# A decoder layer's expert product: output turned, 32 tokens taken by gathers, other packets for gates and activations

## The reference, cut to what matters

```python
idx = take(i1, ci // K) * 128 + take(i2, ci % K)         # (token, head, 16)
gate = softmax(sc)
act = gelu(einsum('thed,td->the', u_table[idx], xb))
y = einsum('the,thed->td', gate * act, v_table[idx])
x = x + y
```

## Time and profile before

| | us |
|---|---|
| median of 3 runs | 1489.33 (1485.82 to 1491.83) |
| the profiled execution | 1488.56 |
| its span | 1486.4 |
| TensorE busy | 1458.1 |
| VectorE busy | 1165.9 |
| ScalarE busy | 640.8 |
| GpSimd busy | 681.1 |

### The profile page before, as it was taken

One profiled execution on the slowest core, in us unless ns is written; L12 is line 12 of the kernel. 1 busy time (PEld: TensorE's weight loads), 2 busy tenths in 40 slices (PEclk: granted clock), 3 DMA queues, 4 the chain that ended last, 5 costly groups with the idle time before them and its releaser, 6 DMA issues.

```text
span 1486.4 us, 23381 instructions
## 1 busy us (share of the span) xinstructions
PE 1458.1 (98%) x8069; PEld 1301.4 (88%) x8069; DVE 1165.9 (78%) x2372; ACT 640.8 (43%) x1055; POOL 681.1 (46%) x394
## 2 busy tenths in 40 slices
PE   7999899999999999999999999999999999999998
PEld 6879668888999999999999999888888888888887
DVE  4747563388989999988998888578788778878876
ACT  4463472321433333467777666433332243233221
POOL 2423171233777768865545453134334434433341
PEclk9999999999999999999999999999999999999999
DMA  7400211312689999999999999699999999999993
GB/s 265 149 29 1 113 45 32 114 58 71 192 296 330 317 332 354 417 356 363 371 376 362 356 368 389 218 392 383 379 355 343 354 348 352 346 348 349 354 344 121
DMA packets 183962, 410.29 MB, mean 276 GB/s; under 512 B 12852, under 2 KB 108852, under 8 KB 182360
## 3 DMA queue, kind: packets, MB, share of 16 engines
q1 hardware_dynamic: 142296, 258.46, 49.3%
q0 software_dynamic: 41600, 151.03, 26.9%
HBM read 361.12 MB, written 48.30 MB: 275 GB/s over the span
## 4 chain that ended last, share of the span: by engine, by line
PE 75%; DVE 9%; DMA 9%; POOL 4%; issue 2%; ACT 1%; SPq 0%; DVEq 0%; ACTq 0%; POOLq 0%
PE banks L1996 17%; PE banks L1764 16%; PE banks L2065 12%; PE banks L2064 12%; PE banks L2066 12%; DMA u_rows<-in_u,idx 8%; DVE gate_rows L1623 3%; POOL u_lo L746 3%; DVE u_rows L1568 2%; POOL u_rows L762 2%; DVE u_lo L1551 1%; PE banks L1976 1%; DVE oh L1619 1%; PE banks L1791 1%; PE banks L1836 1%
## 5 line engine op out<-in xcount | busy, mean ns | idle before, releaser
L794 POOL DMA_INDIRECT v_rows<-in_v,idx x128 | 204.2, 1595 | 325.2 <-DVE x_res L1707 273.6
L2064 PE MATMUL banks<-v_hi,w_hi 128*128 128x512 f32 x768 | 298.8, 389 | 0.0
L2066 PE MATMUL banks<-v_hi,w_lo 128*128 128x512 f32 x768 | 298.8, 389 | 0.0
L2065 PE MATMUL banks<-v_lo,w_hi 128*128 128x512 f32 x768 | 298.8, 389 | 0.0
L1125 ACT ACTIVATE v_hi<-v_raw 128x1024 fp32r<-128x1024 f32 x128 | 126.3, 1050 | 326.1 <-PE banks L2066 298.5
L762 POOL DMA_INDIRECT u_rows<-in_u,idx x160 | 189.8, 1186 | 138.7 <-DVE z L1568 107.4
L1645 DVE TENSOR_TENSOR v_lo<-v_raw,v_hi 128x1024 fp32r<-128x1024 f32 x128 | 153.5, 1221 | 96.5 <-ACT v_hi L1125 96.3
L746 POOL TENSOR_TENSOR u_lo<-u_raw,u_hi 128x1024 fp32r<-128x1024 f32 x66 | 163.8, 2485 | 87.6 <-ACT u_hi L1011 53.7
L1996 PE MATMUL banks<-h_lo,u_hi 128*128 128x352 f32 x1024 | 196.1, 326 | 0.0
L1996 PE MATMUL banks<-h_hi,u_hi 128*128 128x352 f32 x1024 | 188.3, 326 | 0.0
L1996 PE MATMUL banks<-h_hi,u_lo 128*128 128x352 f32 x1024 | 184.7, 323 | 3.3 <-DVE u_lo L1551 3.3
(11 more groups left out here) (276 smaller groups left out, 2078.1 us busy)
## 6 DMA issues: line engine op xcount, KB each, us to landing
u_raw<-in_uT SPq DMA_DIRECT2D x128, 512.0 KB
v_raw<-in_v SPq DMA_DIRECT2D x128, 512.0 KB
gate_scratch<-stage SPq DMA_DIRECT2D x12, 2048.0 KB
gates<-gate_scratch SPq DMA_DIRECT2D x29, 768.0 KB
act_scratch<-act_out SPq DMA_DIRECT2D x116, 176.0 KB
act_in<-act_scratch SPq DMA_DIRECT2D x29, 704.0 KB, 7.4
wi_raw<-in_w_in SPq DMA_DIRECT2D x8, 1024.0 KB, 6.7
wq_raw<-in_w_q SPq DMA_DIRECT2D x8, 1024.0 KB, 6.0
```

The lines of the kernel that those rows point to most:

```text
L794: nc.gpsimd.indirect_dma_start(v_rows[s % V_ROWS][:], None, v_flat, bass.IndirectOffsetOnAxis(ap=idx0[:, s:s + 1], axis=0)).then_inc(vg_in ...
L2064: mm(y, w, v_hi[q][:, j, ds], start=first and j == 0, stop=False)
L2065: mm(y, w, v_lo[q][j][:, ds], start=False, stop=False)
L2066: end = mm(y, w_lo[q][:, j, t * P:(t + 1) * P], v_hi[q][:, j, ds], start=False, stop=last and j == GROUP - 1)
```

## The change

The second product is turned. Before, a matmul had 128 tokens of `w` as the stationary operand and 512 columns of v as the moving one, and gave tokens by width. Now 128 columns of v are stationary and 352 tokens of `w` move, and each of 8 banks holds one eighth of the width by tokens. At the end ScalarE copies the banks to `yT`, TensorE transposes them, and VectorE adds them to the residual.

The 32 tokens leave the dense part: 32 more tiles of v rows are gathered (kind "w"), scaled and accumulated in `acc_b`, four slots of a token in four partition groups, and `fold` sums these groups in eight matmuls into the first 32 columns of the banks. Gates are made for 352 tokens in 88 batches and 11 chunks, and the scaling of the gate table is gone, as is the save of the 32 tokens' chunk in the second product.

All gathers form one order (`ORDER`: dots a and b, then w, then v), with row tiles by address: 3 in turn for the first 12 tiles of v rows, then 6. The first four w tiles are added between the last blocks' splits, the other 156 tiles over groups 1 to 30, five or six a group.

Gates come in pairs of groups (1,024 bytes a piece), into `gate_pairs`, from the group `KEPT` on. Activations are saved by two blocks and loaded as pieces of 2,816 bytes. In the main stage VectorE makes the one-hot rows of all batches and five of the eight gate rows of two batches; ScalarE makes the other three, as a Square and a Relu each, with the gate as bias and the negated gate (`neg_g`) as scale. The output of the three token tiles leaves in six half tiles instead of three whole ones.

```diff
-BATCHES = ND // BATCH
+BATCHES = NA // BATCH
...
+for _n in range(POST + 4, E_BLOCKS):
+    DOTS[_n] = "w" * POST_ADDS
...
+ALL_DOTS += "w" * (NE - ALL_DOTS.count("w")) + "v" * SLOTS
...
+def adds_of(g):
+    return g * ADDS_LEFT // ADD_GROUPS - (g - 1) * ADDS_LEFT // ADD_GROUPS if g <= ADD_GROUPS else 0
...
+        WIDE, MAIN, POST_KB, LATE = (110, 114, 195, 199, 38, 42, 46, 50), (110, 114, 195, 199), (150, 110, 114), (134, 138, 177)
...
+            def save_acts(i, body, pair):
+
+                half = pair % 2
+                sp.wait_ge(act_ready, i * body + (2 * pair + 2))
+                sp.dma_start(act_d[bass.ds(i * (body // 2) + pair, 1)].rearrange("o p n t -> (o p) (n t)"),
+                             act_out[:, 2 * half:2 * half + 2, :].rearrange("p n t -> p (n t)")
+                             ).then_inc(act_saved[half], 16)
...
+            sp.wait_ge(tri_ready, 2 * (TB - 1) + 1)
+            for y in range(P // NE):
+                sp.dma_start(g1[y * NE:(y + 1) * NE, :], tri[0:NE, 0, 0, y * NE:(y + 1) * NE]).then_inc(g1_in, 16)
...
+            def load_pair(block, m, count=2 * GROUP):
+                sp.dma_start(gate_pairs[m][:, :, 0:count, :].rearrange("p c n t -> p c (n t)"),
+                             gate_d[:, :, bass.ds(block, count), :].rearrange("c p n t -> p c (n t)")
+                             ).then_inc(pairs_in[m], 16)
...
+                if s == U_DOTS:
+
+                    pool.wait_ge(gate_saved[1], 16 * (CHUNKS // 2))
+                if s == U_LATE:
+
+                    pool.wait_ge(z_done, E_BLOCKS)
...
-                for w in range(BATCH):
-                    at_t = tab[:, 2, bass.ds(token(i, b, w), 1)]
-                    nc.scalar.activation(oh2[:, slot, w, :], iota, ACT.Square, bias=at_t, scale=-1.0
+                for w in range(ROWS_DVE, BATCH):
+                    at_t = tab[:, 1, bass.ds(token(i, b, w), 1)]
+                    nc.scalar.activation(gate_rows[:, slot, w, :], iota, ACT.Square, bias=at_t, scale=-1.0
...
-                nc.scalar.activation(oh2[:, slot, :, :], oh2[:, slot, :, :], ACT.Relu, bias=1.0, scale=-1.0
-                                     ).then_inc(oh_scalar, 1)
+                for w in range(ROWS_DVE, BATCH):
+                    t = bass.ds(token(i, b, w), 1)
+                    last = nc.scalar.activation(gate_rows[:, slot, w, :], gate_rows[:, slot, w, :], ACT.Relu,
+                                                bias=tab[:, 0, t], scale=neg_g[:, t])
+                last.then_inc(oh_scalar, 1)
...
+            for c in range(KD):
+                act.wait_ge(y_done, c + 1)
+                copy(yT[:, c, :], ps[:, Y_BANKS[c], 0:ND]).then_inc(yT_ready, 1)
...
+                if kind == "w" and x == 0:
+                    nc.vector.tensor_scalar(acc_b[:], rows[:], z1[:, 0:1], None, ALU.mult).then_inc(dot_done, 1)
+                    return
+                w, into = (z1, acc_b[:]) if kind == "w" else (z0, x_res[:, 0, :])
+                nc.vector.scalar_tensor_tensor(out=into, in0=rows[:], scalar=w[:, x:x + 1], in1=into,
+                                               op0=ALU.mult, op1=ALU.add).then_inc(dot_done, 1)
...
-                if n % 2 == 0:
-                    nc.vector.tensor_tensor(oh2[:, slot, :, :], bc(iota, 1, BATCH),
-                                            bc(tab[:, 2, t0:t0 + BATCH], 2, NK), ALU.is_equal).then_inc(oh_ready, 1)
-                for t in range(t0, t0 + BATCH):
+                t0 = n * BATCH + NE
+                nc.vector.tensor_tensor(oh2[:, slot, :, :], bc(iota, 1, BATCH),
+                                        bc(tab[:, 2, t0:t0 + BATCH], 2, NK), ALU.is_equal).then_inc(oh_ready, 1)
+                for t in range(t0, t0 + (ROWS_DVE if n % 2 else BATCH)):
...
-                        step(nc.vector.transpose(z1t[:], z1[:]))
-                        settle()
-                        step(nc.vector.tensor_tensor(tab[:, 0, 0:NE], tab[:, 0, 0:NE], z1t[:], ALU.mult))
...
-            dve.wait_ge(dot_done, len(ORDER))
+            dve.wait_ge(dot_done, U_DOTS)
             weights(0, 0)
+            post_dots(POST + 4)
             split_u(POST + 5)
             split_w(0, 0)
+            post_dots(POST + 5)
             split_u(POST + 6)
+            post_dots(POST + 6)
             split_u(POST + 7)
...
-                for o in range(6):
-                    t, half = divmod(o, 2)
...
+                for c in range(KD):
...
+                    if last and c == 6:
+                        turn(0, range(4))
+                    if last and c == 7:
+                        turn(1, (4, 5))
+                    ds = slice(c * P, (c + 1) * P)
+                    y = ps[:, Y_BANKS[c], NE:ND]
                     for j in range(GROUP):
...
+                        mm(y, v_hi[q][:, j, ds], w_hi[q][:, j, :], start=first and j == 0, stop=False)
+                        mm(y, v_hi[q][:, j, ds], w_lo[q][:, j, :], start=False, stop=False)
+                        end = mm(y, v_lo[q][j][:, ds], w_hi[q][:, j, :], start=False, stop=last and j == GROUP - 1)
...
+            pe.wait_ge(dot_done, U_DOTS + NE)
+            for c in range(KD):
+                mm(ps[:, Y_BANKS[c], 0:NE], acc_b[:, c * P:(c + 1) * P], fold[:], start=False, stop=False)
             second(GROUPS - 1, 1, last=True)
```

More of the change, by code:

```diff
@@ new lines, in second @@
+                if not isinstance(p, int) or KEPT <= p + 2 < GROUPS:
+                    load_act(p + (2 - KEPT), q)
+            for p in range(4):
+                second(p, p % 2, p)
+            with sp.Fori(1, GROUPS // 4 - 1) as i:
+                for r in range(4):
+                    second(i * 4 + r, r % 2, r)
+            for p in range(GROUPS - 4, GROUPS):
+                second(p, p % 2, p % 4)
+            sp.wait_ge(dot_done, GATHERS)
+            sp.dma_start(a["out"][0:P, :], x_res[:, 0, :]).then_inc(out_saved, 16)
@@ L679, in _ @@
+            for o in range(6):
+                half, t = o // 3, 1 + o % 3
+                ds = slice(half * 512, (half + 1) * 512)
+                sp.wait_ge(y_added, o + 1)
+                sp.dma_start(a["out"][t * P:(t + 1) * P, ds], x_res[:, t, ds]).then_inc(out_saved, 16)
+            sp.wait_ge(out_saved, 16 * 7)
         @block.gpsimd
@@ L1099, in main @@
                     n = i * MAIN_BODY + (PRE + j)
-                    take_gates(i, 2 * j, first)
-                    if not (last and j == MAIN_BODY - 1):
+                    if not last or i * MAIN_BATCHES + 2 * j < BATCHES:
+                        take_gates(i, 2 * j, first)
+                    if not last or i * MAIN_BATCHES + 2 * j + 3 < BATCHES:
                         one_hot(i, 2 * j + 3)
@@ L1648, in weights @@
             def weights(g, q):
[L1649 removed]
+                if g < KEPT:
+                    dve.wait_ge(gates_in[q], (g - q) * 8 + 16)
+                    gate = gates[q][:]
+                else:
+                    m, half = divmod(g - KEPT, 2)
+                    dve.wait_ge(pairs_in[m % 2], m // 2 * 16 + 16)
+                    gate = gate_pairs[m % 2][:, :, half * GROUP:(half + 1) * GROUP, :]
                 if g:
@@ L2041, in main, with turn @@
                                 lambda b=b: gate_matrices(i, b, first and b < 4))
-                               for b in BATCHES_IN[j]]
+                               for b in BATCHES_IN[j] if not last or i * MAIN_BATCHES + b < BATCHES]
                     first_product(i * MAIN_BODY + (PRE + j), j, i, PRE + j, MAIN_BODY, between=between)
             main(0, True)
-            with pe.Fori(1, MAIN_TRIPS) as i:
+            with pe.Fori(1, MAIN_TRIPS - 1) as i:
                 main(i)
+            main(MAIN_TRIPS - 1, last=True)
             for n in range(POST, E_BLOCKS):
                 first_product(n, n, 0, n, 1, ring=2)
+            def turn(half, chunks):
+                for c in chunks:
+                    pe.wait_ge(yT_ready, max(c + 1, 3 * half + 3))
+                    for t in range(3):
+                        o = ps[:, Y_BANKS[3 * half + t], c % 4 * P:(c % 4 + 1) * P]
+                        end = nc.tensor.transpose(o, yT[:, c, t * P:(t + 1) * P], ident)
+                        if c % 4 == 3:
+                            end.then_inc(yT_turned, 1)
             def second(g, q, first=False, last=False):
```

248 lines of the change are left out of this document (115 added, 133 removed).

## The result

The kernel became slower by about half a per cent: 1499.59 us, median of 16 runs (1491.73 to 1503.77), against 1490.36 for the kernel before (16 runs, 1485.82 to 1497.13) on the same chip. The ratio is 1.0058, 95% interval 1.0044 to 1.0073. I had forecast 1462 with a range of 1448 to 1482: wrong in sign, and outside the range. The median lies 4.8 us above the profiled execution, where the forecast allowed 0.8; the profiles don't show what the slower executions add.

A forecast was written before the change was run, and what follows sets the result against it. TensorE and DMA were both near full in the second product, with DMA taking over as limit after the change; 1486.4 - 7.1 + 2 - 35.9 + 8 + 5.4 = 1458.8 us of span, forecast 1462, range 1448 to 1482.

The forecast's parts named there:

- the DMA limit of the second product: Second product: DMA queues at 395 GB/s, 15.9 us a group, start group 31 8 us later than TensorE's pace; bounds 0, 24.
- Case 2: Second product: DMA, VectorE and row buffers hold each other up; 1477 at 16.0 us a group, 1486 at 16.3; chance 0.2.
- Case 1: Second product: TensorE sets the pace throughout, larger packets lift the DMA ceiling to 412 GB/s; 1454 to 1446; chance 0.2.
- Case 3: Second product: slower through row-tile turnaround from 19.5 us on, 1503, or a 358 GB/s ceiling, 1521; chance 0.1.
- Second product turned: Second product: 96 matmuls at 158.3 ns, 15.20 us a group, 35.9 us less if TensorE sets the pace.
- Stage with gates, -7.1: First product with gate matrices: 88 batches instead of 96 at 0.89 us, 7.1 us less; bounds nothing and 14.6.
- Last eight blocks, +2: First product's last eight blocks: extra VectorE work ahead of u_lo, +1.4 and +0.6 us; bounds 0 and 6.
- End, +5.4: Kernel's end: fold 0.8 us, transposes inside the last group 2.3, longer tail after the last matmul 2.3; bounds 4 and 8.
- Conditions named for failure: Second product: below 382 GB/s means a mis-sized ceiling; forecast fails if first groups stand long or gaps reach 2.6 us.

The follow-up runs named there:

- Experiment 4: Changed kernel with 20 of the 160 row tiles added behind the last group: 1478.66 us, ratio 0.9917 to the kernel before.
- Experiment 5: Changed kernel without the product of v_hi with w_lo, 64 matmuls a group instead of 96, all bytes kept: 1486.97 us, ratio 0.9983 to the kernel before.
- experiment 3: Changed kernel with five row buffers instead of six in the second product: 1495.94 us, ratio 1.0048 to the kernel before.
- Experiment 6: Changed kernel with each two-group gate load made as two transfers, packets of 512 bytes instead of 1 KB: 1528.62 us, ratio 1.0269 to the kernel before.
- experiment 1: Changed kernel loading v blocks of the second product in half their width from the second group on: 1469.76 us, ratio 0.9863 to the kernel before.
- experiment 2: Changed kernel with 28 row tiles of v, every fifth, replaced by tiny transfers, all adds kept: 1472.57 us, ratio 0.9882 to the kernel before.
- experiment 11: Changed kernel with all gathered u row tiles from the fifth block with gates on replaced by 32-byte-a-partition transfers: 1481.97 us, a single execution.
- experiment 7: Changed kernel with 16 of the 160 row tiles added behind the last group: 1481.60 us, ratio 0.9950 to the kernel before.
- experiment 9: Changed kernel with 20 row tiles added behind the last group and none in the first product's last four blocks: 1483.25 us, ratio 0.9946.

## Why the prediction was wrong

**The step that failed is the DMA limit of the second product**, "group 31 starts 479 us into the stage, where TensorE's own pace has it at 31 x 15.2 = 471: 8 us more", with its bounds of 0 and 24. It measured 511.3, so 40 us and not 8. Three errors lie in it.

*The sum over the stage.* I divided the stage's 186.3 MB by the ceiling and let group 31 start 4 us behind the last v tile. The bytes were right, 187.85 MB by the trace from 958 to 1480 us, but the last v tile landed at 1454.1, 495.4 us into the stage and not 475. TensorE had begun group 30 at 1453.0, so that group 31 began at 1470.0, 16 us behind the tile and not 4. Buffers hold tiles for one or two groups only, so queues can't earn in the light groups at the end what they owe in the heavy ones: groups 0 to 27 cost their own bytes at the queues' pace, and the three from 28 to 30 cost TensorE's 15.2 whatever the queues do. TensorE began group 28 at 1422.5, 463.8 us into the stage; less 28 x 16.41 this leaves 4.3 for the start, a remainder that is fitted and was not forecast. By my own 15.9 us a group that is 4.3 + 28 x 15.9 + 3 x 15.2 = 495.1: 16 us above the 479. The view of bytes per group stood in the prediction, beside the sum that I used instead. Experiment 4 shows the same from the other side: equal bytes in all, 0.35 MB fewer a group, 21 us less.

*The rate.* I took 395 GB/s, near a stretch without gate packets. The stage ran at 382 (16.41 us a group), its lower bound: 28 x 0.51 = 14 us. But as a ceiling my 395 was not too high. Full queues moved 398 with the new packets, which is 15.75 us a group. What I put at nothing is that the queues would not be full all the time: the other 0.66 us of the 16.41 are dry spots, 28 x 0.66 = 18 us, more than the whole 14. They come with late loads. SyncE waited 321.5 us of the 420 from 1000 on for the v_lo that frees a v buffer, and a gate load stands behind four v loads in its order. Experiment 5 shows that TensorE does not make the dry spots, and experiment 3 that one row buffer fewer doesn't make the groups longer. Which buffer or order makes them no run isolates.

*The fold.* It runs ahead of group 31, 1.7 us that I had counted in the last group. With it the three make the 32 us.

The Trainium skill says in "Perfetto Trace Analysis", section DMA Optimizations, that transfers below 2 KB carry much overhead each, and that larger ones are the first remedy of a kernel bound by DMA. Experiment 6 agrees, with 17.47 against 16.41 us a group for 512 bytes against 1 KB. The 358 GB/s that the Trainium skill gives in "DMA: Bandwidth & Descriptors", section Specifications, as a core's HBM limit were no limit for this one core: the stage held 383 for 450 us.

**Rivals.** Case 2 (the three hold each other up) named the right place, ScalarE's wait for v tiles, and asked for 16.0 to 16.3 us a group. Experiments 1 and 2 show that VectorE's order alone is not the limit, and experiment 3 that the number of row buffers is not. But its loop, a late tile, a late v_lo, a late v load, fits the dry spots, which are more than half of what a group took above 15.2 us. So it has a part in the result that I gave it no price for beside the ceiling. Case 1 (a ceiling of 412) is out. Case 3's turnaround is out by experiment 3; its side of the result came true through other mechanisms. With four cases and none added to another, 0.09 for slower was too little: I had priced the error of the ceiling, not that of the way of counting, nor a ceiling and dry spots together.

**Second product turned.** 158.3 ns a matmul and 15.20 a group: right within 2%. Where the bytes are few, a group takes 15.11 to 15.31 by its w_lo; the matmuls stand 159 ns apart in experiment 1 and 161 in experiment 2.

**Stage with gates, -7.1.** Measured -4.2 (the last GELU with gates at 918.42, before at 922.64). The scaling step's stall went, but others took its place: 8.7 us above 43.5 blocks of 5.58, as 7.5 before over 47.5. One of them,

```profile
898.34 1.16 PE L2083 MATMUL banks<-gate_rows,oh 128*128 128x128 f32 x8 [2.87 <-DVE gate_rows L1685]
```

looks like a late gate row; behind it is VectorE, which waited 41.0 us for gathered rows from 655 to 923 us, where it had waited 22.9. The result lies between my bound "nothing, since behind 901 the DMA is already full" and the value that I took. That the rows make the stalls is shown by experiment 11 (8.3 us), a single execution.

**Last eight blocks, +2.** Measured +2.5, near the forecast, but its parts are not shown. The GELUs stand 4.00 us apart in the changed kernel's profile against 3.80 before, TensorE's slower pace, which is up to 1.6 over eight blocks and was no part of my term; experiments 5 and 7, at 3.80 and with the four adds, took 39.25 us, 1.5 more than before.

**End, +5.4.** Right: from group 31's start 23.0 us instead of 23.7 without the fold, and the fold 1.7 instead of 0.8.

**Conditions named for failure.** "Less than 382 says the ceiling was mis-sized": it was 383 over 450 us and 382 over the groups, on the edge, and a sign that could not tell a low ceiling from queues that run dry. Gaps of up to 4.5 us came, and with them stretches at half the clock, which I had left unpriced; the clock is 0.97 in two of the windows above. Against the queues' pace they cost little: experiment 5 bounds all of TensorE's own delay at 0.14 us a group, 4 us, within the scatter named there.

## What to carry to other kernels

Faster matmuls gain nothing where another resource was at 0.97: here the 36 us taken off TensorE's time turned into waits, because the same change put 10% more bytes into each group. Where buffers are short, add up a saturated stage group by group, each at the larger of its bytes over the ceiling and the engine's pace, and never all bytes over the ceiling. Then ask whether the queues are fed all the time: look at windows of 1 us and not of 100, since here a mean share of 1.00 hid dry spots that cost as much as the bytes did. And move bytes from the full groups to where the queues idle, which made the same work 1.4% faster than the changed kernel and 0.8% faster than the one before.

## What the hardware showed beyond that

TensorE ran the same 128x352 matmuls at two paces, with the full clock granted both times. Two profiles, the changed kernel and experiment 6, have the same program up to there. Their windows from 655 to 900 us:

```profile
655.00:900.00 245.00, 239.36 (x1697) 238.22 (x1696) 213.94 (x481) 191.31 (x425) 135.34 (x93) 0.99 0.97 365
```

```profile
655.00:900.00 245.00, 245.00 (x1699) 245.00 (x1699) 218.18 (x487) 191.39 (x425) 137.00 (x96) 1.00 0.95 366
```

One stops for 5.6 us, the other never, and both get through the same number of matmuls: batches of gate matrices stand 2.79 us apart in the first and 2.89 in the second, 158 and 167 ns for each matmul between them. The whole of experiment 11's stage ran at 158 ns with a granted clock of 1.00, so the clock that the profile shows does not tell the two apart. In experiments 4 and 9 the pace changed behind a stall in mid-stage, near 733 and 850 us, and held for 100 us and more. What chooses it I don't know. By itself it makes 8.0 us from the first batch to the last, 251.1 in experiment 6 against 243.1 in experiment 11; but the changed kernel, faster with 8.7 us of stalls, took 251.4, so there the slower pace only fills the time of the stalls. A stage's stalls have to be read together with its pace.
